# Gate rows g1 and g2 from a stored transpose and broadcast loads, in place of products of ones with diagonal matrices

## The reference

```
for i in range(DEPTH):
    last = i == DEPTH - 1
    mod = (silu_c @ w_ada[i] + b_ada[i])[:, None, :]
    mod_c = silu_cc @ w_ada[i] + b_ada[i]
    sh1, sc1, g1, sh2, sc2, g2 = jnp.split(mod, 6, axis=-1)
    ...
    f, fc = _token_mixer(u, uc, ...)
    x = _post_norm(DEEPNORM_ALPHA * x + g1 * f, ln1_g[i], ln1_b[i])
    u2 = _layer_norm(x) * (1.0 + sc2) + sh2
    m = _moe(u2 ...)            # layer 0: x and xc together; layer 1: x alone
    x = _post_norm(DEEPNORM_ALPHA * x + g2 * m, ln2_g[i], ln2_b[i])
```

## Time and profile before

| | |
|---|---|
| median of 3 runs | 2620.76 us (2618.77 to 2621.34) |
| profiled execution, span from first to last instruction | 2617.6 us |
| TensorE busy | 2484.3 us, 95% |
| VectorE, ScalarE, GpSimd busy | 982.1, 525.7, 233.6 us |
| DMA | 733.84 MB, mean 280 GB/s |
| granted TensorE clock, mean | 0.989 of full speed |

### The profile page before, as it was taken

How to read it: one execution, slowest core, us unless ns; L and a number is a source line. 1 busy time by engine, 2 the same in 40 slices (tenths; PEclk the granted TensorE clock), 3 DMA queues, 4 the chain that set the end, 5 groups by cost and what they waited for, 6 DMA issues and landing times.

```text
span 2617.6 us, 36012 instructions
## 1 busy us (share of the span) xinstructions
PE 2484.3 (95%) x12508; PEld 1680.1 (64%) x12508; DVE 982.1 (38%) x2221; ACT 525.7 (20%) x1167; POOL 233.6 (9%) x377
## 2 busy tenths in 40 slices
PE   7999999999999999999999799999998999999997
PEld 4878888888875455455545368778885544444443
DVE  1436624548167211111111286545717311111115
ACT  2234511325131111111111213234511000000000
POOL 0000000000000122111112000000000121111110
PEclk9999999999999999999999999999998999999999
DMA  9874445445365999999999674774453999999995
GB/s 329 266 231 142 146 135 166 146 148 173 129 231 208 379 420 409 418 414 394 413 415 398 266 260 147 243 238 153 145 172 112 366 412 396 401 394 395 388 383 235
DMA packets 293667, 733.84 MB, mean 280 GB/s; under 512 B 33366, under 2 KB 208606, under 8 KB 238352
## 3 DMA queue, kind: packets, MB, share of 16 engines
q1 hardware_dynamic: 267120, 681.78, 69.4%
q0 software_dynamic: 26400, 50.07, 5.0%
HBM read 725.62 MB, written 51.54 MB: 297 GB/s over the span
## 4 chain that ended last, share of the span: by engine, by line
PE 69%; DMA 25%; DVE 4%; SPq 1%; issue 1%; ACT 0%; DVEq 0%; ACTq 0%; POOLq 0%
DMA arena<-in_w 23%; PE psum L890 16%; PE psum L1175 14%; PE psum L1102 6%; PE psum L901 5%; PE psum L1317 3%; PE psum L916 3%; PE psum L1187 3%; PE psum L1137 2%; PE psum L1133 2%; PE psum L1355 2%; PE psum L771 1%; PE psum L753 1%; PE psum L1084 1%; PE psum L832 1%; DMA arena<-in_w_in 1%
## 5 line engine op out<-in xcount | busy, mean ns | idle before, releaser
L890 PE MATMUL psum<-arena 128*128 128x256 f32 x1984 | 445.6, 381 | 1.8 <-DMA arena<-in_w_in 1.0
L1175 PE MATMUL psum<-arena 128*128 128x512 f32 x832 | 381.1, 602 | 35.3 <-DMA arena<-in_w 35.3
L890 PEld LDWEIGHTS psum<-arena 128*128 128x128 f32 x1984 | 372.2, 190 | 60.7 <-issue 5.8
L1317 PE MATMUL psum<-arena 128*64 128x256 f32 (+1 forms) x2848 | 337.7, 382 | 21.7 <-DMA arena<-in_w 19.7
L1317 PEld LDWEIGHTS psum<-arena 128*64 128x64 f32 (+1 forms) x2848 | 213.4, 139 | 118.1 <-DMA arena<-in_w 15.8
L1175 PEld LDWEIGHTS psum<-arena 128*128 128x128 f32 x832 | 152.2, 193 | 197.7 <-issue 154.8
L1187 PE MATMUL psum<-arena 128*128 128x512 f32 x440 | 206.3, 612 | 5.9 <-DVE arena L2200 3.2
L1940 DVE SCALAR_TENSOR_TENSOR grow<-psum,par,grow 128x255 f32<-128x255 f32 (+1 forms) x304 | 136.1, 479 | 125.8 <-ACT grow L1531 120.2
L1102 PE MATMUL psum<-arena 128*128 128x256 f32 x768 | 173.2, 379 | 0.0
L2576 POOL DMA_INDIRECT results<-arena,ids x90 | 92.9, 1032 | 861.2 <-DVE arena L2474 469.9
L2474 DVE COPY arena<-psum 128x512 f32<-128x512 f32 x50 | 34.6, 691 | 342.3 <-PE psum L1187 195.3
(11 more groups left out here) (337 smaller groups left out, 2686.8 us busy)
## 6 DMA issues: line engine op xcount, KB each, us to landing
arena<-in_w SPq DMA_DIRECT2D x405, 1024.0 KB, 16.9
arena<-in_w_in SPq DMA_DIRECT2D x92, 1024.0 KB, 5.3
arena<-in_w_ada SPq DMA_DIRECT2D x32, 1024.0 KB, 7.9
arena<-results SPq DMA_DIRECT2D x24, 1024.0 KB, 9.9
arena<-in_w_br_ssm SPq DMA_DIRECT2D x24, 768.0 KB, 4.4
arena<-in_w_ada SPq DMA_DIRECT2D x8, 2048.0 KB, 14.9
arena<-cumulated SPq DMA_DIRECT2D x36, 384.0 KB, 4.2
arena<-in_w_br_four SPq DMA_DIRECT2D x12, 1024.0 KB, 5.2
```

The lines of the kernel that those rows point to most:

```text
L890: last = mm(o[:, a, :], w[:, k, a * P:(a + 1) * P], rhs[:, k, :], start=k == 0, stop=k == ks - 1, skip_group_check=True)
L1175: last = mm(o.rearrange("p (a n) -> p a n", a=2), lhs(k), w[:, k, :, :], start=k == 0, stop=k == KD - 1)
L1317: last = mm(bank[0][c, a * FF:(a + 1) * FF], xTe[0][:, k, c], w13[b][:, k, a, :], start=k == 0, stop=k == KD - 1)
```

## The change

Once per layer, in call 0 and in call 3, TensorE transposes 32 columns of `modc` for both streams (g1, shift 2, scale 2, g2: columns 16 to 48) into 64 rows of 128, ScalarE copies them into `praw`, and SyncE stores them to a new DRAM tensor, one DMA for each stream (`store_modulation`). A row of g1 or g2 is then a contiguous piece of 4 KB there, and one DMA loads it into all partitions of `grow` (`gate_row`, 512 KB written). g1's row is loaded in each full call behind slab ("g2", 2), ahead of step 2's rows; the g2 rows are loaded when the last bank of the out product has been read, behind the modulation matrices of the next layer in layer 0. The diagonal matrices, the products with ones and the copies go.

```
 SyncE
+            def store_modulation(l):
+                sp.wait_ge(s_mod_row, l + 1)
+                for v in range(2):
+                    sp.dma_start(scratch["mod"][l, v], praw[v:64:2, 0, :]).then_inc(s_mod_out, 16)
+            def gate_row(l, v, first, row, landed):
+                src = scratch["mod"][l, v:v + 1, first:first + KD, :].rearrange("a k p -> a (k p)")
+                sp.dma_start(grow[:, row, :], src.to_broadcast([P, D])).then_inc(landed, 16)
+            def first_gate_row(m):
+                l, v, _ = CALLS[m]
+                if m in LATE_CALLS:
+                    store_modulation(l)
+                if m == 1:
+                    sp.wait_ge(s_read["dve"], freed(BANK_NO[(0, "wo", 3)])[1])
+                if l:
+                    sp.wait_ge(e_comb[0], 8)
+                sp.wait_ge(s_mod_out, 32 * (l + 1))
+                gate_row(l, v, 0, 0, t_gr.sem)
             def rows_after(m, kind, j):
+                if (kind, j) == ("g2", 2):
+                    first_gate_row(m)
...
                         modulation(1, j)
+                sp.wait_ge(s_read["dve"], freed(BANK_NO[(m, "wo", 3)])[1])
+                for v in range(nt // 2):
+                    gate_row(l, v, 24, v, s["g2_in"])
                 post_norm_rows(l, "ln2_g", "ln2_b", norm)
 TensorE
                             pe.wait_ge(s_modc, all_modulations(l))
+                            tp(bank[7][0:64, 0:P], modc[:, 16:48, :].rearrange("p j v -> p (j v)"), ident).then_inc(s_mod_tp, 1)
                         for g in range(1, GROUPS):
                             feature_dft(g)
+                            if g == 1 and m in LATE_CALLS:
+                                pe.wait_ge(s_mod_row, l + 1)
                             token_dft(g - 1)
...
-                        for k in range(KD):
-                            pe.wait_ge(t_gd.sem, t_gd.at(m, k + 1))
-                            last = mm(psum[:, 3 + k // 4, (k % 4) * P:(k % 4 + 1) * P], ones, lnx[:, 0, k * P:(k + 1) * P], start=True, stop=True)
-                        last.then_inc(t_ctm.sem, 1)
                         pe.wait_ge(t_mT.sem, t_mT.at(m, 4))
...
                     u2_transposes(1)
-                    g2_rows(0)
                     logits(0)
...
                         next_product(bank[3], j)
-                    g2_rows(1)
                     count_tokens()
...
                     u2_transposes(0)
-                    g2_rows(0)
                     logits(0)
 ScalarE
                             a_(fA[:, g % 2, :, :], psum[:, b0:b0 + 2, 0:2 * FH], ACT.Copy).then_inc(t_f1c.sem, 1)
+                            if g == 0 and m in LATE_CALLS:
+                                act.wait_ge(s_mod_tp, l + 1)
+                                a_(praw[0:64, 0, :], bank[7][0:64, 0:P], ACT.Copy).then_inc(s_mod_row, 1)
...
-                        act.wait_ge(t_ctm.sem, t_ctm.at(m, 2))
-                        a_(grow[:, 0, :], psum[:, 3:5, :].rearrange("p b n -> p (b n)"), ACT.Copy).then_inc(t_gr.sem, 1)
...
-                    g2_copy(0)
                     scores_and_back(0)
 VectorE
-                        for k in range(KD):
-                            V.tensor_scalar(lnx[:, 0, k * P:(k + 1) * P], ident, modc[:, 16 + k, stream:stream + 1], None, ALU.mult).then_inc(t_gd.sem, 1)
...
-                        dve.wait_ge(t_gr.sem, t_gr.at(m, 1))
+                        dve.wait_ge(t_gr.sem, t_gr.at(m, 16))
...
                 def residual(i):
                     t = MOE_TILES[l][i]
+                    if i == 0:
+                        dve.wait_ge(s["g2_in"], of(l, "g2_in", 16 * nt // 2))
```

More of the change, by code:

```diff
@@ L341, in hybrid_block_kernel @@
         msk = carve(4 * NE).rearrange("p (t e) -> p t e", t=4)
-        gdiag = [arena[:, o:o + D] for o in (xTe_at, xTe_at + D)]
         onep = [arena[:, o:o + D].rearrange("p (j q) -> p j q", j=TOPK) for o in (xTe_at, xTe_at + D, ysb_at, ysb_at + D)]
@@ L412, in hybrid_block_kernel @@
         t_f2c = stage("dft_token_ready", 4, 0)
-        t_ctm = stage("cumulated_heads_then_gate_rows_product", 2, 0)
+        t_ctm = stage("cumulated_heads_product", 1, 0)
         t_wo = stage("first_tile_of_out_product", 2, 0)
@@ L432, in hybrid_block_kernel @@
         t_mT = stage("merged", 4, 0)
-        t_gd = stage("gate_diagonals", 8, 0)
-        t_gr = stage("gate_rows_ready", 1, 0)
+        t_gr = stage("gate_row_in", 16, 0)
+        s_mod_tp = sem("modulation_rows_transposed")
+        s_mod_row = sem("modulation_rows_copied")
+        s_mod_out = sem("modulation_rows_stored")
         names = ("u2_normed u2_transposed u2_ready logits routed plan_products placed blocks_ready "
@@ L438, in hybrid_block_kernel @@
                  "router_in shared_in shared_up shared_sil shared_h shared_ht shared_htc shared_y shared_out "
-                 "g2_diag g2_rows g2_ready scores").split()
+                 "g2_in scores").split()
         s = {n: sem(n) for n in names}
@@ L444, in hybrid_block_kernel @@
                  "routed": nt0 // 2, "onehots": 2 * nt0, "u2_ready": KD * nt0, "shared_y": nt0 - 2,
-                 "router_in": 32, "shared_in": 48, "g2_diag": KD * nt0 // 2, "g2_rows": nt0 // 2, "g2_ready": nt0 // 2}
+                 "router_in": 32, "shared_in": 48, "g2_in": 16 * nt0 // 2}
         COUNTED, RANK_TP, TABLE = 1, 2, 3
@@ L1193, in shared_up @@
                         pe.wait_ge(s["shared_in"], of(l, "shared_in", 48))
-                        pe.wait_ge(s["g2_ready"], of(l, "g2_ready", nt // 2))
+                        pe.wait_ge(s_read["dve"], freed(BANK_NO[(2 * l + 1, "wo", 3)])[1])
                     if i >= 2:
@@ L1213, in shared_down @@
                     last.then_inc(s["shared_y"] if i < shared_before else z["down"], 1)
-                def g2_rows(v):
-                    if v == 0:
-                        pe.wait_ge(s_read["dve"], freed(BANK_NO[(2 * l + 1, "wo", 3)])[1])
-                    else:
-                        pe.wait_ge(s["g2_ready"], of(l, "g2_ready", v))
-                    for k in range(KD):
-                        pe.wait_ge(s["g2_diag"], of(l, "g2_diag", v * KD + k + 1))
-                        last = mm(psum[:, k // 4, (k % 4) * P:(k % 4 + 1) * P], ones, gdiag[v][:, k * P:(k + 1) * P], start=True, stop=True)
-                    last.then_inc(s["g2_rows"], 1)
                 def count_tokens():
@@ L1654, in _ @@
                 act.wait_ge(s_modc, all_modulations(l))
-                for v in range(nt // 2):
-                    for k in range(KD):
-                        a_(gdiag[v][:, k * P:(k + 1) * P], ident, ACT.Copy, scale=modc[:, 40 + k, v:v + 1]).then_inc(s["g2_diag"], 1)
                 if nt == 4:
@@ L1667, in _ @@
                     scores_and_back(3)
-                    g2_copy(1)
                 else:
                     u2_copies(0)
-                    g2_copy(0)
                     scores_and_back(0)
@@ L1688, in _ @@
                     shared_out(1)
-                act.wait_ge(s["g2_ready"], of(l, "g2_ready", nt // 2))
                 act.sem_inc(z["xt_act"], 1)
@@ L2317, in one_hot @@
                 def one_hot(i):
-                    if i == 0:
-                        dve.wait_ge(s["g2_ready"], of(l, "g2_ready", nt // 2))
                     link(V.tensor_tensor(onec[i], columns.unsqueeze(1).to_broadcast([P, TOPK, NB]),
@@ L2635 @@
         "y": nc.dram_tensor("results", (len(MOE_TILES[0]) * P * TOPK, D), F32, kind="Internal").ap(),
+        "mod": nc.dram_tensor("modulation_rows", (DEPTH, 2, 32, P), F32, kind="Internal").ap(),
         "g": nc.dram_tensor("gates", (len(MOE_TILES[1]) * P * TOPK, 1), F32, kind="Internal").ap(),
```

5 lines of the change are left out of this document (removed).

## The result

The changed kernel took 2626.57 us (median of 12 executions, 2620.63 to 2633.6), the kernel before 2621.34 us beside it on the same chip (12 executions): a ratio of 1.0020, 95% interval 1.0013 to 1.0028, or 3.4 to 7.3 us slower. In a later set of executions the same two stood at 2623.96 and 2622.89 us: a ratio of 1.0005, interval 0.9996 to 1.0014. My forecast was 2621.6 us in a range of 2616.5 to 2627.0, so both medians lie in the range, the first by only 0.4 us. The likeliest case, "within 0.2%", sits on its edge in the first comparison and holds in the second.

What follows compares the result with a forecast made beforehand. TensorE's chain (69%) was taken as the bound, with DMA at 25%. Terms -3.7 (expert start), +0.2 (transposes), +2.3 (call 0) and +2.0 (call 3) sum to +0.8 us: 2621.6 us, range 2616.5 to 2627.

Steps and rivals of the forecast that it cites:

- within 0.2%: Whole kernel: a time between 2615.5 and 2626.0 us, no change a measurement can tell; chance 0.78.
- Layer 0's expert start: Start of layer 0's expert part: without both g2 product groups, gain 1.7 + 2.0 = 3.7 us.
- Ends of calls: End of each full call: g1 products filled TensorE's wait for VectorE's last merge, so removing them gains 0 us.
- Layer 1's expert start: Start of layer 1's expert part: products and copy precede TensorE's 2.88 us idling for the second norm; 0 us.
- The transposes: One added per late call between two Fourier products: 0.11 us each, 0.2 us for both calls.
- The stores' landing: SyncE's queue in call 0: stores land at 243.0 us, half a microsecond after slab g2/2; bounds 242.5 and 245.1.
- Call 0: Step 2 of the state-space part: rows 4.1 us later, of which 2.3 us reach TensorE; low 1.0, high 4.8.
- the 4 us at which I had said that I am wrong: Sign in calls 0 and 3: forecast wrong if the delayed state-space step grows by over 4 us; 2 us expected.
- Call 3: State-space part, VectorE taken as its bound: late rows cost 2.0 us; low 0.7, high 4.5.
- Call 1: No store here; gate row issued while SyncE waits anyway: 0 us, at most 0.3.
- How much reaches TensorE?: Call 0, step 2: 4.1 us delay less 0.92 and 1.2 slack, plus 0.3 restart, gives 2.3 us.
- a rival on the clock: Layer 0's expert start, tile-3 logits: clock fall spared, about 3 us more gained, 2618.6 us; chance 0.08.

Runs made afterwards that it cites:

- a version made for this test: Stores early in calls 0 and 3, plus layer 0's two stores and their wait repeated in call 1; 2623.82 us against 2622.28 for the kernel before.
- The version whose expert start was not earlier: The change with stores early and the g2 rows made by products again, only g1 from DRAM; 2622.97 us, ratio 1.0007 to the kernel before.

## Why the prediction was right, and where it was not

**The forecast held in place, and in size where the clock did not fall.** The parts, without falls of the clock, add up to +1.9 us where I had +0.8, and 1.2 of the 1.9 is the loop, where I had nothing. The first median, +5.2, is in the range by 0.4 us, and that is luck: the top of the range had been drawn for stores that land late, and what filled it was falls of the clock and the loop, for which the sum had no term.

- *Layer 0's expert start,* -3.7: measured -3.4 and -3.7, and undoing it alone brings it back. In the first trace the tile-3 logits start 1.6 us sooner and the counts 3.6, where I had 1.7 and 3.7. Whether VectorE's tile-3 norm would cap a larger gain no run shows.
- *Ends of calls,* 0: measured 0.0 in every version, and restoring the products cost nothing. The reason, VectorE's merge, is in the chain, and TensorE's gap ahead of the out product is 1.51 us, as I had written down.
- *Layer 1's expert start,* 0: up to 0.9 of either sign, less than the 1.6 between the two traces of the kernel before; TensorE idles for VectorE's norm as before.

```profile
2003.80 1.09 PE L873 MATMUL psum<-cst,arena 128*128 128x128 f32 x8 [2.97 <-DVE arena L1765]
```

  This is the timeline's row that answers to the earlier trace rows: 2.97 us of idling against 2.88. I had written that this idling becomes longer, and it hardly does. The 2 us of the products went into a wait that I hadn't named, for ScalarE's copies: TensorE now idles 0.70 us ahead of the tile-0 logits, and these last 2.79 us in place of 1.90.
- *The transposes,* 0.2: 0.10 and 0.11.
- *The stores' landing* stood in my sum 5.7 us after the slab's issue; measured 5.85. The Trainium skill ("DMA: Bandwidth & Descriptors", "Anatomy of one DMA") with its 2 us a transfer had made me weigh 1.5 us more. That section describes transfers that GpSimd issues, and these are SyncE's. The trace shows no 2 us behind the slab: it landed at 242.2, and the last store was seen 0.5 us after it. What such a store takes with no slab ahead of it no run shows.
- *Call 0,* 2.3 for the stall: 2.6. The 4.1 us of delay were 4.2 (12.32 against 8.16). With the falls the step grew by 5.6 and 4.1 us in the two traces of the change, over the 4 us at which I had said that I am wrong.
- *Call 3,* 2.0: 1.4. The rows landed 12.2 us after the slab's issue, where I had 11.6, and still cost less: ScalarE's path led, and its start moved by 5.1 us (12.2, against 7.1 from the earlier trace rows), so it had 3.7 us of slack. I had taken VectorE's head for the measure.
- *Call 1,* 0: measured 0.

**The step that failed** is "How much reaches TensorE?": I priced the idling by its length. In two of three traces of the full stall in call 0 the granted clock fell behind it and took 1.5 and 3.0 us more, and in call 1, in a version made for this test, 1.7. I had a rival on the clock, but looked for it only at the expert start, where the earlier trace rows showed it already, and there only for a gain. A new idling of nearly 2 us needed the same question.

**The second miss** is the expert loop. I had 0 there. All twelve traces of changed versions lose 0.8 to 2.0 us between 842.75 and 1460.70 us, the two of the kernel before 0 and -0.3. The version whose expert start was not earlier loses it as well, so the gain isn't just absorbed by the loads. Nearly all of it stands in one wait. TensorE idles ahead of the group at 1460.70 us (L1175, L1198 in the changed file); the kernel before, its second trace, and the change:

```profile
1460.70 3.70 PE L1175 MATMUL psum<-arena 128*128 128x512 f32 x8 [0.55 <-DMA arena<-in_w]
1459.69 3.70 PE L1175 MATMUL psum<-arena 128*128 128x512 f32 x8 [0.30 <-issue]
1464.23 5.39 PE L1198 MATMUL psum<-arena 128*128 128x512 f32 x8 [2.47 <-DVE arena L2462]
```

The idling is 1.5 to 2.5 us in all twelve changed versions' traces, and at 1440 us, just ahead of this place, the shift of each is within 0.5 us of what it was at 842.75. The VectorE instruction that the row names does not explain it by itself: in the change it ends at 1463.25, and TensorE starts 0.98 us later. Which of the parts that all versions share (the transpose, the stores, some row load, the new tensor's place in memory, the changed program text) causes it was not tried; it stays open.

## What to carry to other kernels

Before a store and its wait go into a queue that issues loads, look for a place where this queue waits anyway: the same round trip cost 4 us in two calls with the stores at (g2, 2), and nothing with the stores one slab earlier. Here products on the chain were worth about their length, and products that hid another engine's last step were worth nothing, and both look alike in the sum of busy time. When a change makes TensorE idle for a time that it didn't before, price it once by its length and once with a fall of the clock behind it, and take more than one trace: here one execution had none, another 3 us.

## What the runs showed of the hardware that I had not expected

The fall of the clock behind an idling is not fixed by the program. Behind 1.9 us of idling (1.85 and 1.86) at the same instructions the granted clock stayed at 1.00, or stood near 0.50 for 3.3 us, or for 6.3; behind 3.0 us in call 1 it fell in the one trace, behind 1.4 to 1.5 us in call 3 it did not in three. The Trainium skill ("TensorE: Matmul & The Clock Gate", "Part 1: The HAM clock gate") says that the same kernel shows the change at another point from run to run, since the phase of the gate is not tied to the program. The three traces of call 0 agree in that the fall comes or not from run to run; that the phase is the reason they don't show. In the tail of layer 0's expert part whole groups were 1.7 us longer or not, from execution to execution, 5.9 us in all. Two stores of 16 KB right behind a 1 MB slab took 4.4 to 5.1 us from issue to landing in call 0 and were seen 0.2 and 0.5 us after the slab, which itself took 5.3. Moved early and issued 3.4 us behind another slab, which took 4.6, they took 1.7 and 1.8. So most of the wait is for the slab ahead in the queue rather than for their 16 KB.
